# Down-projections' last unit summed earlier, raw products first at the beginning, and x copied by ScalarE

## The chip, the cores and the metric

The kernel runs on one core of a Trainium2 chip. The metric is the device time of one execution in microseconds. Three runs of the kernel before took 2900.92, 2905.70 and 2906.11 us; their median is 2905.7.

The engines go by the profile's names: PE is TensorE (PEld its loading of weights), DVE is VectorE, ACT is ScalarE, POOL is GpSimd, SP is SyncE, which issues nearly all loads.

## What is computed

x is 256 tokens of 1024 features in float32. Three blocks of a network follow each other: two layers of a conformer (convolution, then stick-breaking attention), a block with two kinds of attention, and a block with attention, a state-space branch and a mixture of experts. The change touches only the very first step of the program and the four feed-forward halves of the first block:

```python
def swiglu_ffn(h, w_in, w_out):
    gate, up = jnp.split(h @ w_in, 2, axis=-1)
    return (jax.nn.silu(gate) * up) @ w_out

def first_block(x, ...):
    for i in range(2):
        x = x + 0.5 * swiglu_ffn(rms_norm(x, g[0]), ffn_w_in[i, 0], ffn_w_out[i, 0])
        ...  # convolution (i = 0) or attention (i = 1)
        x = x + 0.5 * swiglu_ffn(rms_norm(x, g[2]), ffn_w_in[i, 1], ffn_w_out[i, 1])
```

w_in is 1024 x 5632 and w_out 2816 x 1024.

## The kernel before, in words

A plan of stages is run by every engine in the same order; the engines meet only at semaphores. x is held transposed in `xT`: 128 features by 256 tokens, eight such chunks. `Setup` loads x, lets PE transpose it into four banks (`turned` counts the banks, two chunks each), and DVE copies each bank into `xT` (L346), which raises `x_done`. For each pair of chunks `Norm.step` on DVE scales them by the gains into `hR` (L420, `h_ready`), and `Norm.act` on ACT squares them into `hT` (L411, `sq_ready`); `Norm.gather` (L428) adds the squares, `Norm.sum` is PE's sum over the partitions (L472), and its root and reciprocal give `rstd`.

Weights come through a ring of four slots. SP issues a unit's load as soon as PE has released the slot, which `w_used` counts, unit after unit through all stages.

`SevenUp` computes h @ w_in with seven products of half-sized blocks in place of eight. It takes 11 units of 2 MB. For each, DVE forms four sums of quarters of the weights (`combine`, L896 to L899, 128 x 1024 each; the last raises `combined`), and once per stage four sums of x's quarters (`take_turns`, L908 to L911; `turns`). A unit is two output chunks of 7 products each; a product is four matmuls of 128 x 128 by 128 columns in float32, and each matmul shows as two records in the trace. P1 and P2 read the weights and `hR` as they are; P3 reads a sum of weights and raw x; P6, P5, P7 and P4 read what was made of both (their tiles are `wrow`, `drow`, `hR` and `both`). In the first unit PE waits for the weights and for `combined`, then runs P1, P2 and P3 of both chunks, waits for `turns`, and runs the other four, with `Norm.sum` between the chunks.

`SevenDown` does the same for the second product, with 5 units of two pairs of chunks and a last one (unit 5) of one pair. `prepare` (L1192 to L1199) forms for unit j four sums of x's side and four of the weights'. It waits for the unit's load, for `w_used` of unit j - 2, whose work space it takes, and for the hidden chunks. For unit 5 the space is another: `drow`, `wrow`, `both` and the area from column 6144 on of `wk`. DVE prepares units 0 and 1 within the up-projection and 2 to 5 in `SevenDown.dve`, one behind the other. PE runs units 0 to 3 one by one; then it waits for units 4 and 5 both and takes them together, product by product, and `plus` (L1219) and L1227 to L1236 add each finished product to x behind it. In the second of the four down-projections an up-projection comes next but one, and DVE forms the sums of its unit 0 (`ahead`) after unit 5's; they lie in the space of unit 3.

DVE's first sums for the four up-projections start at 15, 358, 565 and 933 us, and its sums for unit 5 of the four down-projections at 211, 561, 776 and 1136 us.

Of the kernel before, what the change touches and what calls it, by code (L numbers as in the profile page):

```python
# [36 lines left out]
ACT, ALU, AX = mybir.ActivationFunctionType, mybir.AluOpType, mybir.AxisListType.X  # L37
# [197 lines left out]
class Stage:  # L235
# [11 lines left out]
    def banks_left(self, pe):  # L247
        pass
# [46 lines left out]
    def pe(self, pe):  # L295
        pass

    def act(self, act, chain):
        pass

    def dve(self, dve, chain):
        pass
# [5 lines left out]
class Setup(Stage):  # L308
# [16 lines left out]
        sp.dma_start(k.con[:, 0:FIRST], k.arg["constants"][:, 0:FIRST]).then_inc(self.ones_loaded, 16)  # L325

    def act(self, act, chain):
        k = self.k
        act.dma_start(k.par[:, :], k.arg["params"]).then_inc(k.par_loaded, 16)

    def pe(self, pe):
        k, nc = self.k, self.k.nc
# [9 lines left out]
    def dve(self, dve, chain):  # L342
        k, nc = self.k, self.k.nc
        for b in range(4):
            dve.wait_ge(self.turned, b + 1)
            nc.vector.tensor_copy(k.xT[:, 2 * b:2 * b + 2, :], pair(k.bank[:, 4 + b, :])).then_inc(k.x_done, 1)  # L346
            if b == 0:
                dve.wait_ge(k.par_loaded, 16)
            self.then.step(dve, chain, b)
        self.then.up.late = 1  # L350
        self.then.up.ahead(dve, chain)
        for n, (a, b) in enumerate((("final_g", "attn_norm_2"), ("final_norm_2", "norm_mix_w_3"))):
            chain(nc.vector.tensor_tensor(k.gains[:, n * KC:(n + 1) * KC], k.p(a, 0, KC), k.p(b, 0, KC), ALU.mult))


def pair(ap):
    return ap.rearrange("p (a n) -> p a n", a=2)
# [17 lines left out]
class Norm(Stage):  # L375
# [30 lines left out]

    def act(self, act, chain):
        k, nc = self.k, self.k.nc
        for b in range(4):
            act.wait_ge(k.x_done, self.x0 + b + 1)  # L410
            nc.scalar.activation(self.sq(b), k.xT[:, 2 * b:2 * b + 2, :], ACT.Square).then_inc(self.sq_ready, 1)  # L411
        act.wait_ge(self.mean_ready, self.at(self.mean_ready, 1))
        nc.scalar.activation(k.rstd[:, :], k.rstd[:, :], ACT.Sqrt).then_inc(self.root_ready, 1)

    def step(self, dve, chain, b):

        k, nc = self.k, self.k.nc
        dve.wait_ge(k.x_done, self.x0 + b + 1)
        for c in (2 * b, 2 * b + 1):
            last = nc.vector.tensor_scalar(k.hR[:, c, :], k.xT[:, c, :], self.g(c), None, ALU.mult)  # L420
        last.then_inc(self.h_ready, 1)
        if b >= 2:
            self.gather(dve, chain, b - 1)
# [265 lines left out]
class GatedUp(Stage):  # L689
# [56 lines left out]
    def t(self, n):  # L746
        a = (n % 4) * 2 * S
        return pair(self.k.wk[:, a:a + 2 * S])
# [26 lines left out]
class SevenUp(GatedUp):  # L775
# [25 lines left out]
    def s(self, j, n):  # L801
        a = (j % 2) * self.SW + (n if n < 3 else 2) * 1024
        return self.quarter(j, 0, 1) if n == 2 else self.k.wk[:, a:a + 1024].rearrange("p (c n) -> p c n", c=4)

    def b(self, half, t):
        return self.k.hR[:, 4 * half:4 * half + 4, t * P:(t + 1) * P]
# [26 lines left out]

    def pe(self, pe):
        k, nc, norm = self.k, self.k.nc, self.norm
        raw, made = (self.P1, self.P2, self.P3), (self.P6, self.P5, self.P7, self.P4)

        def products(n, which):
            j, m = n // 2, n % 2
            f = self.factors(j)  # L840
            for p in which:
                a, b = f[p]
                for c in range(4):
                    last = nc.tensor.matmul(k.bank[:, 2 * (n % 4) + p // 4, (p % 4) * P:(p % 4 + 1) * P],  # L844
                                            a[:, c, m * P:(m + 1) * P], b[:, c, :], start=c == 0, stop=c == 3)
            return last

        for j in range(self.UNITS):
            pe.wait_ge(self.loaded(j), self.loads(j))
            pe.wait_ge(self.combined, self.at(self.combined, j + 1))  # L850
            if j == 0:
                if self.at(self.scaled, -2) > 0:
                    pe.wait_ge(self.scaled, self.at(self.scaled, -2))
                for b in range(2):
                    norm.h_waits(pe, 2 * b)
                for m in range(2):
                    products(m, raw[:1])
                for b in range(2, 4):
                    norm.h_waits(pe, 2 * b)
                for m in range(2):  # L860
                    products(m, raw[1:])
                pe.wait_ge(self.turns, self.at(self.turns, 1))
                products(0, made).then_inc(self.up_ready, 1)
                norm.sum(pe)
                products(1, made).then_inc(k.w_used, 1)
                continue
            for m in range(2):
                n = 2 * j + m
                if self.at(self.scaled, n - 3) > 0:
                    pe.wait_ge(self.scaled, self.at(self.scaled, n - 3))  # L870
                if n == 2:
                    pe.wait_ge(norm.mean_ready, norm.at(norm.mean_ready, 1))
                products(n, raw + made).then_inc(k.w_used if m else self.up_ready, 1)
# [219 lines left out]
class SevenDown(Project):  # L1093
# [92 lines left out]
    def prepare(self, dve, chain, j):  # L1186

        v, a, b, t, s = self.k.nc.vector, self.quarter, self.b, self.turn, self.s
        dve.wait_ge(self.loaded(j), self.loads(j))
        dve.wait_ge(self.k.w_used, self.used(j - 2))  # L1190
        dve.wait_ge(self.by.hid_done, self.by.at(self.by.hid_done, FC // 2 + 2 * j + self.n(j)))
        chain.mark(v.tensor_tensor(t(j, 0), b(j, 0, 1), b(j, 0, 0), ALU.subtract))  # L1192
        chain(v.tensor_tensor(s(j, 0), a(j, 0, 1), a(j, 1, 1), ALU.add))
        chain.mark(v.tensor_tensor(t(j, 2), b(j, 1, 1), b(j, 0, 1), ALU.subtract))
        chain.mark(v.tensor_tensor(t(j, 1), b(j, 1, 1), t(j, 0), ALU.subtract))
        chain.mark(v.tensor_tensor(s(j, 2), a(j, 0, 0), a(j, 0, 1), ALU.subtract))
        chain(v.tensor_tensor(s(j, 1), s(j, 0), a(j, 0, 0), ALU.subtract))
        chain.mark(v.tensor_tensor(t(j, 3), b(j, 1, 0), t(j, 1), ALU.subtract))
        chain(v.tensor_tensor(s(j, 3), a(j, 1, 0), s(j, 1), ALU.subtract), self.made)  # L1199
# [13 lines left out]
    def dve(self, dve, chain):  # L1213
        k, v = self.k, self.k.nc.vector
        p1, u3, u4 = (self.sum(n) for n in range(3))
        x11, x12, x21, x22 = (k.xT[:, 4 * c:4 * c + 4, t * P:(t + 1) * P] for c in range(2) for t in range(T))

        def plus(out, p, x):
            return v.scalar_tensor_tensor(out, self.out(p), self.scale, x, ALU.mult, ALU.add)  # L1219

        for j in range(2, self.UNITS):
            self.prepare(dve, chain, j)
        if self.then.up:
            self.then.up.late = 1
            self.then.up.ahead(dve, chain)
        dve.wait_ge(self.p1_taken, self.at(self.p1_taken, 1))
        chain.mark(v.tensor_tensor(x11, x11, p1, ALU.add))  # L1227
        dve.wait_ge(self.out_ready, self.at(self.out_ready, 2))
        chain(plus(u3, self.P6, p1))
        dve.wait_ge(self.out_ready, self.at(self.out_ready, 3))  # L1230
        chain.mark(plus(u4, self.P5, u3))
        dve.wait_ge(self.out_ready, self.at(self.out_ready, 4))
        chain(plus(u3, self.P7, u3))
        chain.mark(v.tensor_tensor(x22, x22, u3, ALU.add))
        chain.mark(v.tensor_tensor(x21, x21, u3, ALU.add))
        chain(v.tensor_tensor(x12, x12, u4, ALU.add))  # L1236
        chain.mark(plus(x22, self.P5, x22))
        dve.wait_ge(self.out_ready, self.at(self.out_ready, 5))
        chain.mark(plus(x12, self.P3, x12))
        dve.wait_ge(self.out_ready, self.at(self.out_ready, 6))  # L1240
        plus(x11, self.P2, x11).then_inc(k.x_done, 2)
        self.then.step(dve, chain, 0)
        self.then.step(dve, chain, 1)
        dve.wait_ge(k.w_used, self.used(self.UNITS - 1))
        plus(x21, self.P4, x21).then_inc(k.x_done, 2)
        self.then.step(dve, chain, 2)
        self.then.step(dve, chain, 3)
# [1133 lines left out]
class SubNorm(Stage):  # L2381
# [29 lines left out]
    def square(self, act, chain):  # L2411
        k, nc = self.k, self.k.nc
        self.heads_out(act)
        chain(nc.scalar.activation(k.big[:, 0:8, :], k.big[:, 16:24, :], ACT.Square), self.squared)
# [1003 lines left out]
```

## Time and profile before

| | us |
|---|---|
| median of three runs | 2905.7 |
| the profiled execution | 2901.93 |
| its span | 2900.10 |
| PE busy | 2799.3 (97%) |
| DVE busy | 1421.7 (49%) |
| ACT busy | 472.2 (16%) |
| mean granted clock of PE | 0.988 |

All times below are counted from the start of the span. A timeline row gives start and duration, the engine and line, the operation with the tile it writes and those it reads, how many were merged, and in brackets the engine's idle time before it with what ended it. In the 40 slices of the page PE is at 9 tenths in nearly all; DMA is at 3 to 6 tenths until about 2220 us and at 9 from there on, in the stage of the experts.

### The profile page before, as it was taken

What the parts mean: (1) busy time and instruction counts of PE and PEld (TensorE: products, weight loads), DVE (VectorE), ACT (ScalarE), POOL (GpSimd) and SP (SyncE); (2) the same over time, 40 slices, a digit from 0 to 9 for tenths busy, and PEclk for the clock granted to TensorE, in tenths of its full rate; (3) what the DMA queues carried; (4) which work ended last, traced back from release to release, by engine and by line L of the source; (5) the groups of instructions that cost most, each with busy time, mean ns of one, the idle gap of its engine ahead of it and who ended that gap; (6) DMA issues with size and microseconds to landing.
All of it is one profiled execution on the core that took longest, in us unless ns stands there. A gap on an engine that the chain in (4) does not pass through costs nothing. (4 is left out here: it accounts for less than half of the span.)

```text
span 2900.1 us, 41051 instructions
## 1 busy us (share of the span) xinstructions
PE 2799.3 (97%) x17281; PEld 2264.6 (78%) x17281; DVE 1421.7 (49%) x2726; ACT 472.2 (16%) x953; POOL 0.2 (0%) x4
## 2 busy tenths in 40 slices
PE   7999899999999999999999999999997999999998
PEld 7998799999988999888888888888885434434343
DVE  7767687588555775542035337466103222223232
ACT  1001410010043100222010012344201000101001
POOL 0000000000000000000000000000000000000000
PEclk9999999999999999999999999999998999999999
DMA  7644155355354443546544444554553999999996
GB/s 225 207 151 151 46 162 175 131 175 174 117 131 146 157 164 113 133 113 156 155 145 147 158 109 110 155 144 125 138 156 136 427 426 426 426 426 427 425 427 288
DMA packets 370294, 594.80 MB, mean 205 GB/s; under 512 B 15680, under 2 KB 327264, under 8 KB 347488
## 3 DMA queue, kind: packets, MB, share of 16 engines
q1 hardware_dynamic: 365344, 588.01, 57.6%
q10 hardware_dynamic: 4800, 4.63, 0.6%
q8 instruction: 114, 1.87, 0.3%
q14 instruction: 36, 0.29, 0.0%
HBM read 591.52 MB, written 1.08 MB: 204 GB/s over the span
## 5 line engine op out<-in xcount | busy, mean ns | idle before, releaser
L3139 PE MATMUL bank<-ring,wk 128*64 128x512 f32 x1408 | 312.9, 597 | 6.0 <-DMA ring<-in_w_expert_gate 6.0
L844 PE MATMUL bank<-hR,ring 128*128 128x128 f32 x2112 | 267.9, 277 | 10.6 <-DVE wk L899 9.0
L3139 PEld LDWEIGHTS bank<-ring,wk 128*64 128x64 f32 x1408 | 99.8, 138 | 212.1 <-issue 212.1
L844 PEld LDWEIGHTS bank<-hR,ring 128*128 128x128 f32 x2112 | 252.8, 194 | 11.6 <-issue 9.4
L3236 DVE TENSOR_TENSOR hT<-bank,hT 128x512 f32<-128x512 f32 x92 | 63.6, 691 | 313.4 <-PE bank L3126 311.0
L3165 PE MATMUL bank<-big,wk 128*64 128x512 f32 x352 | 155.8, 595 | 15.1 <-ACT wk L3196 15.1
L733 PE MATMUL bank<-hR,ring 128*128 128x256 f32 x704 | 152.3, 379 | 0.0
L1157 PE MATMUL bank<-big,ring 128*128 128x128 f32 x1056 | 134.7, 284 | 15.6 <-DVE wk L1199 15.6
L733 PEld LDWEIGHTS bank<-hR,ring 128*128 128x128 f32 x704 | 133.8, 190 | 18.2
L2251 PE MATMUL bank<-big,ring 128*128 128x256 f32 x640 | 141.1, 379 | 1.5 <-ACT big L2733 1.0
L1157 PEld LDWEIGHTS bank<-big,ring 128*128 128x128 f32 x1056 | 129.3, 201 | 16.3 <-issue 16.3
L1038 PE MATMUL bank<-big,ring 128*128 128x256 f32 x608 | 134.5, 384 | 4.9 <-ACT big L1409 4.3
L2251 PEld LDWEIGHTS bank<-big,ring 128*128 128x128 f32 x640 | 121.4, 190 | 18.3 <-ACT big L2733 1.2
L1038 PEld LDWEIGHTS bank<-big,ring 128*128 128x128 f32 x608 | 116.9, 193 | 21.7 <-issue 4.7
L3165 PEld LDWEIGHTS bank<-big,wk 128*64 128x64 f32 x352 | 46.4, 137 | 108.3 <-issue 88.0
L2298 DVE TENSOR_TENSOR wk<-bank,wk 128x512 f32<-128x512 f32 x16 | 11.1, 692 | 216.8 <-ACT wk L2290 216.8
L1515 PE MATMUL bank<-hR,ring 128*128 128x256 f32 x512 | 114.5, 382 | 0.1
L2251 PE MATMUL bank<-hT,ring 128*128 128x256 f32 x512 | 113.3, 379 | 0.0
L2636 PE MATMUL bank<-hT,ring 128*128 128x256 f32 x512 | 113.0, 381 | 0.0
L1515 PEld LDWEIGHTS bank<-hR,ring 128*128 128x128 f32 x512 | 96.5, 191 | 13.9 <-DVE hR L420 0.9
L2636 PEld LDWEIGHTS bank<-hT,ring 128*128 128x128 f32 x512 | 97.2, 191 | 12.9
L2251 PEld LDWEIGHTS bank<-hT,ring 128*128 128x128 f32 x512 | 97.0, 190 | 13.0
(429 smaller groups left out, 4571.2 us busy)
## 6 DMA issues: line engine op xcount, KB each, us to landing
ring<-in_ffn_w_in SPq DMA_DIRECT2D x88, 1024.0 KB
ring<-in_w_expert_gate SPq DMA_DIRECT2D x44, 2048.0 KB
ring<-in_w_expert_up SPq DMA_DIRECT2D x44, 2048.0 KB
ring<-in_w_in SPq DMA_DIRECT2D x96, 512.0 KB
big<-in_w_expert_down SPq DMA_DIRECT2D x44, 1024.0 KB
ring<-in_ffn_w_out SPq DMA_DIRECT2D x40, 1024.0 KB
ring<-in_w_up SPq DMA_DIRECT2D x22, 1024.0 KB
hR<-in_w_expert_down SPq DMA_DIRECT2D x22, 1024.0 KB
```

Of the source, the lines that this page charges most:

```text
L733: last = nc.tensor.matmul(k.bank[:, n % 4, h * S:(h + 1) * S], w[:, c, h * 256 + m * P:h * 256 + (m + 1) * P], k.hR[:, c, :], start=c == 0 ...
L844: last = nc.tensor.matmul(k.bank[:, 2 * (n % 4) + p // 4, (p % 4) * P:(p % 4 + 1) * P], a[:, c, m * P:(m + 1) * P], b[:, c, :], start=c == ...
L1038: return k.nc.tensor.matmul(k.bank[:, self.banks[o // 2], (o % 2) * S:(o % 2 + 1) * S], w[:, c, o * P:(o + 1) * P], self.src[:, n, :], sta ...
L1157: last = k.nc.tensor.matmul(k.bank[:, self.BANK[p], m * P:(m + 1) * P], a[:, i, m * P:(m + 1) * P], b[:, i, :], start=j + i + m == 0, stop ...
L1515: last = nc.tensor.matmul(k.bank[:, bank, n * S:(n + 1) * S], w[:, c, n * P:(n + 1) * P], self.h[:, c, :], start=c == 0, stop=c == KC - 1)
L2251: last = nc.tensor.matmul(out, v[:, q, :], src[:, q, :], start=q == 0, stop=q == chunks - 1)
L2298: chain(nc.vector.tensor_tensor(k.wk[:, 3072:3072 + 2 * S], k.bank[:, 2 * (c % 2) + 1, :], both, ALU.mult))
L2636: last = nc.tensor.matmul(k.bank[:, n // 2, (n % 2) * S:(n % 2 + 1) * S], w[:, c, n * P:(n + 1) * P], k.hT[:, c, :], start=c == 0, stop=c ...
L3139: last = nc.tensor.matmul(k.bank[a:a + SLOTS, 2 + n, :], xg[:, c * P + a:c * P + a + SLOTS], self.weights(j, c, KC), start=c == 0, stop=c ...
L3165: last = nc.tensor.matmul(k.bank[a:a + SLOTS, 5 + h, :], ht[:, c * P + a:c * P + a + SLOTS], self.weights(j, c, 4)[:, h * 512:(h + 1) * 51 ...
L3236: return v.tensor_tensor(x, k.bank[:, self.PUT_BANKS[n], :], x, ALU.add)
```

## The change

Three edits:

- `Setup`: ACT copies the four banks into `xT` instead of DVE and squares each pair of chunks right behind its copy. The squares of this first norm move out of `Norm.act` into `Norm.square`; for all later norms nothing changes.
- `SevenUp.pe`, first unit: the wait for `combined` moves behind P1 and P2 of both chunks; P3 of both chunks follows it, then the wait for `turns` as before.
- `SevenDown.prepare`: unit 5 doesn't wait for `w_used` of unit 3 any more. Where sums for the next up-projection follow, this wait stands ahead of them instead.

```diff
 class Setup
     def act(self, act, chain):
-        k = self.k
+        k, nc = self.k, self.k.nc
         act.dma_start(k.par[:, :], k.arg["params"]).then_inc(k.par_loaded, 16)
+        for b in range(4):
+            act.wait_ge(self.turned, b + 1)
+            nc.scalar.activation(k.xT[:, 2 * b:2 * b + 2, :], pair(k.bank[:, 4 + b, :]), ACT.Copy).then_inc(k.x_done, 1)
+            self.then.square(act, b)
...
     def dve(self, dve, chain):
         for b in range(4):
-            dve.wait_ge(self.turned, b + 1)
-            nc.vector.tensor_copy(k.xT[:, 2 * b:2 * b + 2, :], pair(k.bank[:, 4 + b, :])).then_inc(k.x_done, 1)
...
 class Norm
     def act(self, act, chain):
-        for b in range(4):
-            act.wait_ge(k.x_done, self.x0 + b + 1)
-            nc.scalar.activation(self.sq(b), k.xT[:, 2 * b:2 * b + 2, :], ACT.Square).then_inc(self.sq_ready, 1)
+        if self.x0:
+            for b in range(4):
+                self.square(act, b)
...
+    def square(self, act, b):
+        act.wait_ge(self.k.x_done, self.x0 + b + 1)
+        self.k.nc.scalar.activation(self.sq(b), self.k.xT[:, 2 * b:2 * b + 2, :], ACT.Square).then_inc(self.sq_ready, 1)
...
 class SevenUp
     def pe(self, pe):
-        raw, made = (self.P1, self.P2, self.P3), (self.P6, self.P5, self.P7, self.P4)
+        raw, made = (self.P1, self.P2), (self.P3, self.P6, self.P5, self.P7, self.P4)
...
         for j in range(self.UNITS):
             pe.wait_ge(self.loaded(j), self.loads(j))
-            pe.wait_ge(self.combined, self.at(self.combined, j + 1))
-            if j == 0:
+            if j:
+                pe.wait_ge(self.combined, self.at(self.combined, j + 1))
+            else:
...
                 for m in range(2):
                     products(m, raw[1:])
+                pe.wait_ge(self.combined, self.at(self.combined, 1))
+                for m in range(2):
+                    products(m, made[:1])
                 pe.wait_ge(self.turns, self.at(self.turns, 1))
-                products(0, made).then_inc(self.up_ready, 1)
+                products(0, made[1:]).then_inc(self.up_ready, 1)
                 norm.sum(pe)
-                products(1, made).then_inc(k.w_used, 1)
+                products(1, made[1:]).then_inc(k.w_used, 1)
...
 class SevenDown
     def prepare(self, dve, chain, j):
-        dve.wait_ge(self.k.w_used, self.used(j - 2))
+        if j < self.UNITS - 1:
+            dve.wait_ge(self.k.w_used, self.used(j - 2))
...
     def dve(self, dve, chain):
         if self.then.up:
             self.then.up.late = 1
+            dve.wait_ge(k.w_used, self.used(self.UNITS - 3))
             self.then.up.ahead(dve, chain)
```

## Rows read from the trace of the kernel before

**Rows 1.** PE's waits, whole span: in all, times, longest (us)
```profile
PE bank L1157 <- DVE wk L1199: 15.6, 4, 3.9
...
PE bank L844 <- DVE wk L899: 9.0, 1, 9.0
```

**Rows 2.** Timeline, tail of the first down-projection: start, us, what, idle before
```profile
204.24 1.22 DVE L1199 TENSOR_TENSOR wk<-ring,wk 128x1024 f32<-128x1024 f32 x1
...
209.59 1.95 PE L1157 MATMUL bank<-hT,ring 128*128 128x128 f32 x16
211.75 0.29 DVE L1192 TENSOR_TENSOR drow<-big 128x128 f32<-128x128 f32 x1 [6.29 <-PE bank L1157]
...
214.61 0.68 DVE L1199 TENSOR_TENSOR wk<-ring,wk 128x512 f32<-128x512 f32 x1
...
221.61 1.06 PE L1157 MATMUL bank<-wrow,wk 128*128 128x128 f32 x8
```

**Rows 3.** One us of that tail: length, PE busy (records), clock, DMA share, GB/s
```profile
217.00:218.00 1.00, 1.00 (x7) 0.50 1.10 353
```

**Rows 4.** Timeline of PE, tails of the second and the fourth down-projection
```profile
559.62 1.95 PE L1157 MATMUL bank<-hT,ring 128*128 128x128 f32 x16
...
571.44 1.06 PE L1157 MATMUL bank<-wrow,wk 128*128 128x128 f32 x8
572.33 1.95 PE L1157 MATMUL bank<-hT,wk 128*128 128x128 f32 x16
...
1134.39 1.95 PE L1157 MATMUL bank<-hT,ring 128*128 128x128 f32 x16
...
1147.21 1.06 PE L1157 MATMUL bank<-wrow,wk 128*128 128x128 f32 x8
```

**Rows 5.** Window in the first down-projection: PE, PEld, DVE, ACT, POOL, clock, DMA, GB/s
```profile
193.00:196.00 3.00, 3.00 (x30) 3.00 (x29) 0.00 (x0) 0.00 (x0) 0.00 (x0) 1.00 0.00 0
```

**Rows 6.** Timeline of the beginning, Setup and first up-projection
```profile
8.69 0.69 DVE L346 COPY xT<-bank 128x512 f32<-128x512 f32 x1 [8.69 <-PE bank L338]
9.41 0.63 ACT L411 ACTIVATE hT<-xT 128x512 f32<-128x512 f32 x1 [6.95 <-DVE xT L346]
...
15.22 1.22 DVE L896 TENSOR_TENSOR wk<-ring 128x1024 f32<-128x1024 f32 x1
...
20.20 5.46 PE L844 MATMUL bank<-hR,ring 128*128 128x128 f32 x24 [8.99 <-DVE wk L899]
...
23.31 0.69 DVE L911 TENSOR_TENSOR both<-hR,wrow 128x512 f32<-128x512 f32 x1
...
28.28 1.06 PE L844 MATMUL bank<-wrow,wk 128*128 128x128 f32 x8
...
36.29 1.95 PE L844 MATMUL bank<-hR,ring 128*128 128x128 f32 x16
```

**Rows 7.** Window over PE's first products, columns as in group 5
```profile
20.20:25.70 5.50, 5.50 (x26) 5.50 (x27) 5.26 (x9) 0.00 (x0) 0.00 (x0) 1.00 1.10 349
```

**Rows 8.** ACT's copy of a whole bank, in the tail of group 2
```profile
219.68 0.60 ACT L1211 ACTIVATE wk<-bank 128x512 f32<-128x512 f32 x1 [39.18 <-PE bank L1157]
```

**Rows 9.** DMA queue of the loads, first 13 us: packets, MB, share
```profile
q1 hardware_dynamic: 2629, 3.41, 79.0%
```

**Rows 10.** Timeline of PE, two gaps elsewhere
```profile
298.37 30.50 PE L1348 MATMUL bank<-wk,hR 128*128 128x256 f32 x140 [1.36 <-DVE wk L1422]
...
1768.91 0.55 PE L1782 MATMUL bank<-con,wk 128*128 128x128 f32 x3 [1.98 <-DVE wk L1844]
```

**Rows 11.** Clock behind the second of them, columns as in group 3
```profile
1770.00:1772.00 2.00, 2.00 (x9) 0.50 1.20 303
```

**Rows 12.** SyncE's queue: the first load of the experts' weights
```profile
2222.91 1.07 SPq L3105 DMA_DIRECT2D ring<-in_w_expert_gate  x2
```

**Rows 13.** ACT: a table load, and a copy behind a square root
```profile
14.62 1.28 ACT L413 ACT_TABLE_LOAD   x1
...
33.77 0.26 ACT L880 ACTIVATE wk<-bank 128x128 f32<-128x128 f32 x1
```


## The prediction

> **What bounds the kernel now.** The page comes first: PE is by far the busiest engine, so a change pays only where PE stands idle or runs slowly. The next view is PE's list of waits. Its first entry is PE's products of the down-projections waiting for the last DVE sum (L1199): 15.6 us in 4 times, none over 3.9; its third is one wait of 9.0 us of the first up-projection for L899 [rows 1]. The change touches these two and nothing else on that list. The granted clock comes third, for what a wait costs besides itself.
>
> **The last unit of each down-projection, before.** PE ends unit 3 of the first one 1.95 us after 209.59, at about 211.5. DVE has been idle 6.29 us, and only then begins unit 5's eight sums: the first at 211.75, the last (0.68 us) at 214.61 [rows 2]. PE waits 3.90 us, since it takes units 4 and 5 together. The wait costs more than that. In the 218th us the granted clock is 0.50, that is 1.2 GHz instead of 2.4, after PE had been idle; PE then starts 7 matmul records in a us [rows 3]. So I take the whole cost from starts. From the last group of unit 3 (16 records) to the first product on wrow, past P1 (24) and P6's first half (16), are 56 records; at the steady pace, where 8 records take 0.89 us (571.44 to 572.33 [rows 4]), they need 56 x 0.1115 = 6.25 us. They took 221.61 - 209.59 = 12.02 here [rows 2], 571.44 - 559.62 = 11.82 in the second down-projection and 1147.21 - 1134.39 = 12.82 in the fourth [rows 4]; the third repeats the first to 0.01. The losses are 5.77, 5.57, 5.78 and 6.57, together 23.7 us: 15.6 of wait and 8.1 of half clock and restart. The granted clock is half in all four.
>
> **The same after.** Unit 5's eight sums no longer wait for unit 3's products. Unit 4's last sum begins at 204.24 and takes 1.22, so DVE is free at 205.46. The block lasted from 211.75 to 215.29 = 3.54 us, so it ends near 209.1, 2.4 us ahead of 211.5 [rows 2]. It stands beside unit 3's products in DVE's 6.29 us of idle time and costs nothing; if that cover were gone, PE would wait for what sticks out beyond 2.4 us. Its other conditions hold: unit 5's weights follow unit 1's release, and between 193 and 196 us the DMA engines stand still, all issued loads landed, before unit 4's sums begin [rows 5] (the three others look the same there); the last hidden unit is DVE's own earlier work, by the order of its code. No DMA is moved and SP's queue is passed by nothing. What is late next in the tail is PE itself, 28 products of unit 4 and as many halves of unit 5. I take the full 23.7; the lower bound is the waits alone, 15.6.
>
> The second down-projection has a further edit: the sums for the next up-projection (combine of its unit 0), until now behind unit 5's, get a wait of their own for unit 3's products. Behind it on DVE stand these four sums and then the first addition to xT. Before, they followed unit 5's last sum, on which PE's restart waits too. After, they begin at unit 3's end, which is PE's start of the tail: the same distance. P6's end (24 + 24 records, 5.4 us into the tail) comes later than theirs (4 sums of 1.22, as at L896 [rows 6], 5.0 with their waits), so DVE is back in step by the sum after it. Nothing for it.
>
> **The first up-projection, before.** The transposes end at 11.2. DVE copies x, scales it, adds squares, and starts unit 0's sums (combine, L896) at 15.22, straight behind its own L428; they end at 20.10. PE waits 8.99 us and starts at 20.20 [rows 6]. It runs P1, P2, P3 for both halves (48 records), waits for nothing, and starts the made products on wrow at 28.28; the turns of x (L908 to L911) had ended at 24.00. Unit 1 starts at 36.29 [rows 6]. From 20.2 to 25.7 PE starts 26 records in 5.5 us [rows 7], where 49 would fit at 0.1115 each, so the first stretch is at half speed although its granted clock is printed as 1.00. I therefore trust starts over the printed clock. The Trainium skill, "TensorE: Matmul & The Clock Gate", section "Part 1: The HAM clock gate (the "warmup" mystery)", warns that recorded clock events can be unreliable, and says that the slow state is the default and activity ends it. This row agrees with both; by the printed clock the slow stretch would not exist and an earlier start would gain more than I count.
>
> **The same after, step by step.** (a) ACT now copies x. A 128x512 copy out of a bank takes it 0.60 us [rows 8], its square 0.63, DVE's copy 0.69 [rows 6]. With about 0.05 for each wait a round is 1.3 us: the fourth copy ends at 8.69 + 3 x 1.3 + 0.6 = 13.2, DVE scales (0.62) and adds (0.68) to 14.6 and starts the sums 0.6 us earlier than at 15.22. The bounds: 0 if ACT's waits eat it, 2.7 (four DVE copies) if ACT were free. I take 0.6, since ACT's pace sets it. (b) The weights of unit 0: by 13.0 us queue q1 has moved 3.41 MB [rows 9]; x, the first constants and two 1.05 MB halves are 3.28 MB. So they are there at about 13, before DVE needs them. (c) PE starts P1 at about 13 and P2 after 13.9; these 32 records need 7.3 us at half speed, so they end between 17 and 20.3. The sums are ready at 19.5; P3 (16 records, 1.8 us) ends between 21.3 and 22.1. (d) Then PE waits for the turns, at 24.00 - 0.6 = 23.4. (e) From the first made product to unit 1 it took 36.29 - 28.28 = 8.0, so unit 1 starts at 31.4: 4.8 us earlier. (f) PE now meets a gap of 1.3 to 2.1 us that it did not have. A gap of 1.98 us before 1768.91 [rows 10] was followed by half clock [rows 11], and so was one of the same length at 246.7; one of 1.36 [rows 10] was not. The price of one such stretch is 5.57 - 3.90 = 1.7 us. I take it, by the rows nearest to 2 us: the start gives 4.8 - 1.7 = 3.1. Its bounds are 0 and 4.8 plus the 2.1 that DVE's copies could add at best.
> Behind it DVE's second combine ends at 28.92 - 0.6 = 28.3, before 31.4, and rstd moves with it. The other three up-projections have their sums before PE asks: there only the order of P2 and P3 changes, at no cost.
>
> **Whether the gain reaches the end.** In the last stage, the experts, DMA is nearly full by the page's slices. But its first load is issued at 2222.91 [rows 12], once the stages before are through, so this stage starts earlier as a whole, and its length stays.
>
> **The sum.** 23.7 + 3.1 = 26.8 us. The profiled execution took 2901.93, span 2900.10; it becomes 2875.1. The median of the three runs shown is 3.8 above it, and I predict for the median: 2905.7 - 26.8 = 2878.9 us.
>
> **Rivals.**
>
> R1, the clock holds at the start: the gap is nearer 1.3 than 2.1. For: P1 and P2 may be slow to the end; against: the two gaps near 2. Sum 23.7 + 4.8 = 28.5: 2877.2.
> R2, only the waits go: half clock comes in the tails anyway, from something other than the gap. Against: all four stretches lie at the gap and PE runs at 1.00 on both sides. Sum 15.6 + 3.1 = 18.7: 2887.0.
> R3, ACT loads a table at each change between copy and square: 7 changes x 1.28 us [rows 13] = 9.0 put the turns at 32.4 and unit 1 at 40.4, so the start loses 4.1: 23.7 - 4.1 = 19.6, 2886.1. Against: a copy follows a square root at 33.77 with no load between [rows 13]. The Trainium skill, "ScalarE: Activation LUTs", says that copy is in every table set; the trace agrees there.
> R4, the edit in the tails does nothing, since another condition holds unit 5's sums until unit 3 ends. DVE's wait in the trace is for PE, and the loads are done early, so little speaks for it. Sum 3.1: 2902.6.
> R5, slower: a PE without these pauses is granted half clock more often. It would sit in the dense stretch to 1161 us. The price is half of each us at 1.2 GHz; it decides from 54 us of additional half clock (26.8 lost), and 66 of it give 33 lost: 2911.9. Against: PE runs undisturbed at 1.00 for long dense stretches today.
>
> **How the numbers follow.** Forecast 0.47, R1 0.25, R2 0.12, R3 0.07, R4 0.03, R5 0.02; 0.04 for other small gaps that shift and move some half-clock stretch by 1.7 us either way. Runs of the kernel before spread 5.2 us (2900.92 to 2906.11). The range 2870 to 2888 takes in R1 less one spread, R2 and R3, and leaves out R4 and R5. About 0.2% (5.8 us) is what a measurement of this kernel can tell from no change; faster by more than that 0.95 (all but R4, R5), same 0.03, slower 0.02.
>
> **What the profile after would show.** In the tails: drow's sum near 205.5 - 4.8 in DVE, no PE wait for L1199, granted clock 1.00 there, 6.3 us from the last group of unit 3 to wrow. At the start: PE's first product near 13, a wait of PE for L911 of 1.3 to 2.1 us, unit 1 at 31.4 (33.1 with half clock); ACT without table loads between its copies. The prediction is wrong if a wait of over 1 us for L1199 stays, if the clock is half in the tails, or if the gain is there at 1160 us and gone at 2230.

## The result and the profile after

The median went from 2903.76 us (four runs, 2900.92 to 2906.11) to 2878.65 us (four runs, 2876.68 to 2878.84). The ratio is 0.9912 with a 95% interval of 0.9895 to 0.9930: faster, by 25.1 us. The prediction was 2878.9 us, in a range of 2870 to 2888. The profiled execution took 2876.68 us and its span 2874.9, 25.2 less than before, where the sum had said 26.8. In one more series, on another occasion, the changed kernel's median was 2876.41 (2874.79 to 2878.20) against 2901.24 before.

First the waits of PE. Of the two entries that the change was about [rows 1], the tails' 15.6 us are gone from the list. In place of the 9.0 us stand two shorter waits in the first up-projection: 2.3 us for the scaled x (L427) and 1.9 us for the turns (L922). Columns: in all, times, longest.

```profile
PE bank L851 <- DVE hR L427: 3.9, 4, 2.3
PE bank L1795 <- DVE wk L1857: 3.8, 2, 2.0
...
PE bank L851 <- DVE both L922: 2.5, 4, 1.9
```

**The tails.** The timeline of the first down-projection after, the same places as [rows 2] (L1204 and L1211 are L1192 and L1199 of before, L1168 is L1157):

```profile
199.22 1.22 DVE L1211 TENSOR_TENSOR wk<-ring,wk 128x1024 f32<-128x1024 f32 x1
200.47 0.29 DVE L1204 TENSOR_TENSOR drow<-big 128x128 f32<-128x128 f32 x1
...
203.34 0.69 DVE L1211 TENSOR_TENSOR wk<-ring,wk 128x512 f32<-128x512 f32 x1
...
204.56 1.95 PE L1168 MATMUL bank<-hT,ring 128*128 128x128 f32 x16
...
206.35 2.84 PE L1168 MATMUL bank<-big,ring 128*128 128x128 f32 x24
...
210.82 1.06 PE L1168 MATMUL bank<-wrow,wk 128*128 128x128 f32 x8
```

Unit 5's sums follow unit 4's last one without a break and end at 204.03. PE ends unit 3 at 206.35 and starts the tail there. From the last group of unit 3 to wrow it now takes 210.82 - 204.56 = 6.26 us, where the sum had 6.25 and before 12.02. The clock holds. Per us: length, PE busy (records), clock, DMA share, GB/s:

```profile
206.00:207.00 1.00, 1.00 (x11) 1.00 0.00 0
...
208.00:209.00 1.00, 1.00 (x11) 1.00 0.63 134
```

**The beginning.** The rows that answer to [rows 6]:

```profile
8.87 0.60 ACT L332 ACTIVATE xT<-bank 128x512 f32<-128x512 f32 x1 [6.39 <-PE bank L342]
9.50 0.63 ACT L420 ACTIVATE hT<-xT 128x512 f32<-128x512 f32 x1
...
12.33 0.58 ACT L332 ACTIVATE xT<-bank 128x512 f32<-128x512 f32 x1
...
13.68 5.47 PE L851 MATMUL bank<-hR,ring 128*128 128x128 f32 x32 [2.29 <-DVE hR L427]
14.30 1.23 DVE L907 TENSOR_TENSOR wk<-ring 128x1024 f32<-128x1024 f32 x1
...
19.23 2.05 PE L851 MATMUL bank<-hR,wk 128*128 128x128 f32 x16
...
22.40 0.69 DVE L922 TENSOR_TENSOR both<-hR,wrow 128x512 f32<-128x512 f32 x1
...
23.15 1.16 PE L851 MATMUL bank<-wrow,wk 128*128 128x128 f32 x8 [1.86 <-DVE both L922]
...
31.26 1.95 PE L851 MATMUL bank<-hR,ring 128*128 128x128 f32 x16
```

ACT copies in 0.60 and 0.58 us and squares behind each copy, the sums start at 14.30 instead of 15.22, PE starts at 13.68 instead of 20.20, the turns end at 23.09 and unit 1 starts at 31.26 instead of 36.29.

**A ledger.** A record of PE in one trace can be set against the same record in another. The table gives by how much a kernel's record starts ahead of that of the kernel before, at seven places: the first product of unit 1 (36.29 in before), the first products behind the four down-projections (235.91, 585.73, 800.49, 1161.50), one in the last block (2041.13), one in the experts (2244.45), and the end of the span. Each row is one profiled execution. The work behind 1161 us is the same in all of them. The record at 2041.13 is the one behind a wait that comes up again below.

| kernel | unit 1 | 236 | 586 | 800 | 1161 | 2041 | 2244 | end |
|---|---|---|---|---|---|---|---|---|
| after | 5.03 | 10.79 | 16.25 | 22.02 | 28.57 | 27.75 | 25.14 | 25.2 |
| after_again | 4.78 | 10.54 | 15.02 | 20.79 | 27.35 | 26.80 | 24.31 | 24.5 |
| after_third | 3.58 | 9.35 | 13.81 | 19.58 | 26.14 | 25.58 | 23.03 | 23.2 |
| tail_only | -0.30 | 5.47 | 11.62 | 17.39 | 23.94 | 23.65 | 23.50 | 23.7 |
| order_only | 4.04 | 2.74 | 2.75 | 2.75 | 2.76 | 2.75 | 2.78 | 3.0 |
| copy_only | 1.55 | 1.54 | 2.13 | 2.13 | 2.12 | 2.35 | 2.17 | 2.4 |
| start_only | 5.20 | 5.20 | 1.45 | 0.64 | 0.26 | 0.00 | -0.12 | -0.1 |
| filled_wait | -0.19 | 1.43 | 3.69 | 5.32 | 7.73 | 7.06 | 6.63 | 6.8 |
| late_sums | 5.21 | 6.41 | 7.46 | 10.30 | 12.38 | 10.41 | 10.21 | 10.4 |
| turns_first | 5.95 | 11.71 | 15.49 | 21.72 | 28.74 | 26.76 | 24.28 | 24.5 |
| later_9 | 3.19 | 8.95 | 13.42 | 19.18 | 25.74 | 25.04 | 24.89 | 24.6 |
| later_18 | 1.02 | 6.78 | 9.95 | 15.71 | 22.27 | 21.64 | 21.48 | 21.3 |
| shifted_code | 5.29 | 11.06 | 17.22 | 22.99 | 29.54 | 28.94 | 28.70 | 28.7 |

The first row already says what the total hides: 28.6 us were gained by 1161 us, and 3.4 of them were lost behind it, in stages that the change doesn't touch.

### The profile page after: what moved, and what is told of

The parts are those of the page before. It is cut to its first block and busy times, and to the rows that moved or that the text cites. A ratio compares the mean times of both kernels' runs of the same rounds, so it can differ in the third digit from the quotient of the medians.

```text
span 2874.9 us, 41046 instructions
## 1 busy us (share of the span) xinstructions
PE 2796.7 (97%) x17281; PEld 2260.9 (79%) x17281; DVE 1419.8 (49%) x2722; ACT 474.7 (17%) x957; POOL 0.2 (0%) x4
## 5 line engine op out<-in xcount | busy, mean ns | idle before, releaser
L2264 PEld LDWEIGHTS bank<-big,ring 128*128 128x128 f32 x640 | 121.4, 190 | 18.3 <-ACT big L2746 1.2
L1049 PEld LDWEIGHTS bank<-big,ring 128*128 128x128 f32 x608 | 116.8, 193 | 21.8 <-issue 4.7
L1168 PE MATMUL bank<-big,ring 128*128 128x128 f32 x1056 | 127.7, 275 | 0.0
L1168 PEld LDWEIGHTS bank<-big,ring 128*128 128x128 f32 x1056 | 122.7, 192 | 0.0
```

Source lines behind the costliest of these rows:

```text
L1049: return k.nc.tensor.matmul(k.bank[:, self.banks[o // 2], (o % 2) * S:(o % 2 + 1) * S], w[:, c, o * P:(o + 1) * P], self.src[:, n, :], sta ...
L1168: last = k.nc.tensor.matmul(k.bank[:, self.BANK[p], m * P:(m + 1) * P], a[:, i, m * P:(m + 1) * P], b[:, i, :], start=j + i + m == 0, stop ...
L2264: last = nc.tensor.matmul(out, v[:, q, :], src[:, q, :], start=q == 0, stop=q == chunks - 1)
```

## The experiments

### The edits one by one

The changed kernel once more, as it is.

> The changed kernel once more, nothing altered. The first traces agree to 0.1 us in which gains have come by where: 5.0 us behind the first up-projection, 28.6 by 1161 us, and then 3.4 are lost by 2250 us. Theory 1 (the loss is chance: half-clock stretches of the second and third block fall differently in each execution): the first two figures repeat within 0.5 us, the loss from 1161 us on comes out otherwise, anywhere from -5 to +5 us. Theory 2 (the loss is the change's, given back later): it is again 3.4 within 0.5 us, with the same half-clock stretches at 1786 and 2015 us.

Unit 1 at 4.78, 27.35 at 1161 us, and then 2.8 lost. The first figure repeats to 0.25, the second only to 1.2 (1.0 of it arose between 236 and 586 us, where the half-clock stretches fell differently), and the loss behind 1161 us is there again, with the half-clock stretch at 2016 us. That spoke for theory 2.

The tails' edit alone:

```diff
 def prepare(self, dve, chain, j):
-    dve.wait_ge(self.k.w_used, self.used(j - 2))
+    if j < self.UNITS - 1:
+        dve.wait_ge(self.k.w_used, self.used(j - 2))
 ...
+        dve.wait_ge(k.w_used, self.used(self.UNITS - 3))
         self.then.up.ahead(dve, chain)
```

> Only the edit of the down-projections. Forecast by the prediction: 23.7 us gained by the end of the fourth, in steps of 5.8, 5.6, 5.8 and 6.6, no PE wait for the last sum in the tails, no half clock there, and nothing gained before 200 us. Rival (only the wait goes, the half clock comes anyway): 15.6. The time is 0.9918 of before if it all lasts, 0.9946 by the rival.

The gains between the places of the table are 5.77, 6.15, 5.77 and 6.55, together 24.2; 0.6 of the second came before its tail, from a shorter half-clock stretch at 337 us. Taken from the last records of unit 3 to the end of the down-projection, the four tails gain 5.77, 5.56, 5.77 and 6.56, together 23.7 as forecast, and the same, within 0.01, in the seven other traces that have this edit and nothing put ahead of unit 5's sums. Only 0.4 is lost later. The ratio is 0.9925 (0.9908 to 0.9941), median 2879.25. The rival of 15.6 is out.

The order of the products alone:

```diff
-        raw, made = (self.P1, self.P2, self.P3), (self.P6, self.P5, self.P7, self.P4)
+        raw, made = (self.P1, self.P2), (self.P3, self.P6, self.P5, self.P7, self.P4)
 ...
-            pe.wait_ge(self.combined, self.at(self.combined, j + 1))
-            if j == 0:
+            if j:
+                pe.wait_ge(self.combined, self.at(self.combined, j + 1))
+            else:
```

> Only the order in the first unit of the up-projections: P1 and P2 ahead of the wait for the sums. DVE still copies x, so the turns are ready at 24.0 as before, and unit 1 starts at 24.1 + 8.0 = 32.1: 4.2 us gained, if the half clock does not follow PE's wait for the turns; 2.5 if it does. Rival (the order brings little by itself, it needs the faster sums): under 1 us.

```profile
13.55 6.68 PE L844 MATMUL bank<-hR,ring 128*128 128x128 f32 x32 [2.28 <-DMA ring<-in_ffn_w_in]
...
24.14 1.16 PE L844 MATMUL bank<-wrow,wk 128*128 128x128 f32 x8 [1.86 <-DVE both L915]
...
32.25 1.95 PE L844 MATMUL bank<-hR,ring 128*128 128x128 f32 x16
```

PE starts its raw products at 13.55, waits 1.86 us for the turns, and unit 1 starts at 32.25: 4.04, where 4.2 were expected. But at the first tail 1.3 of it is given back, and the ratio is 0.9996 (0.9987 to 1.0006).

```profile
212.00:214.00 2.00, 2.00 (x11) 0.50 1.10 349
214.00:216.00 2.00, 2.00 (x11) 0.50 0.65 204
```

The old wait in the tail is still there in this kernel, and half clock behind it lasted 6.8 us from 210.7 on instead of 3.4.

ACT's copy alone:

```diff
 class Setup, def act
+        for b in range(4):
+            act.wait_ge(self.turned, b + 1)
+            nc.scalar.activation(k.xT[:, 2 * b:2 * b + 2, :], pair(k.bank[:, 4 + b, :]), ACT.Copy).then_inc(k.x_done, 1)
+            self.then.square(act, b)
 class Setup, def dve
-            dve.wait_ge(self.turned, b + 1)
-            nc.vector.tensor_copy(k.xT[:, 2 * b:2 * b + 2, :], pair(k.bank[:, 4 + b, :])).then_inc(k.x_done, 1)
```

> Only ACT's copy of x and its squares. The sums end 0.6 to 0.9 us earlier, and PE, which then has only them to wait for, starts 0.6 to 0.9 us earlier; unit 1 starts at 35.4 to 35.7. Rival (the four copies of 0.69 us come off DVE's path in full): 2.7 us.

```profile
19.17 5.04 PE L851 MATMUL bank<-hR,ring 128*128 128x128 f32 x24 [7.88 <-DVE wk L906]
...
34.74 1.95 PE L851 MATMUL bank<-hR,ring 128*128 128x128 f32 x16
```

PE starts 1.03 earlier, a little above the expected 0.6 to 0.9, and reaches unit 1 1.55 earlier; the other 0.5 is that the slow pace at the start of PE's work ended 0.5 us sooner in its run of products (24 records in 5.04 instead of 5.46 us). The rival's 2.7 is out: ACT's rounds of copy and square set the pace. Ratio 0.9996 (0.9987 to 1.0006).

Both edits of the start without the tails':

> The two edits of the start together, without the tails'. Alone the order gave 4.0 and the copy 1.55 us at unit 1; together 5.0 as in the first trace of after (3.5 if half clock follows PE's wait for the turns). By 235 us this may shrink, as the order's 4.0 did to 2.7, since the half clock in the first tail can last 6.8 us instead of 3.4. From 1161 us on: nothing lost if the loss hangs on the time of arrival (this one comes 5 us earlier than before, not 24 to 29), 3 lost if it hangs on the start's edits.

Little of the gain lasts in this trace. The 5.20 at unit 1 are still whole behind the first down-projection, 1.45 behind the second and 0.26 at 1161 us. The loss has two places. The first is the convolution between 236 and 301 us, where 2.6 us go (0.3 comes back at 347 us) and the change alters nothing:

```profile
293.20 33.34 PE L1359 MATMUL bank<-wk,hR 128*128 128x256 f32 x140 [3.07 <-DVE wk L1433]
```

In the kernel before, half clock followed a wait of 1.97 us ahead of 246.71 (from 247.6 on, 3.4 us), and PE then waited 1.36 us at this line [rows 10]. Here no half clock followed the first wait, so PE came to L1359 early, waited 3.07 us for DVE, and half clock of 6.8 us (from 292.2 on) followed that wait. The second place is the tails, whose waits are still four of 3.9. The first tail loses nothing, the other three lose 1.5, 0.8 and 0.4 us against before. In the second and third the half clock is longer:

```profile
562.00:564.00 2.00, 1.46 (x7) 0.50 1.09 360
564.00:566.00 2.00, 2.00 (x11) 0.50 1.07 341
566.00:568.00 2.00, 2.00 (x11) 0.50 0.05 14
```

It lasts 6.8 us at 561.8 and at 776.9, where the trace of before had 3.4 each time. The profiled execution took 2902.0 us, where ten executions lie between 2897.0 and 2903.6; over all of them the ratio is 0.9988 (0.9979 to 0.9998), about 3 us. So the start's gain is real, but how much of it lasts changes from execution to execution with the half clock behind PE's later waits. That is so in the changed kernel too, whose tails have no waits: between 236 us and the second tail after loses 0.1, after_again and after_third lose 1.1. Both of these have the wait of 3.07 us in the convolution, after has 1.38. From 1161 us on start_only loses 0.3, so the start's edits alone don't bring the later loss.

### What a wait costs

In the kernel before, PE's wait in the tails was filled with work that no one reads:

```diff
+        for _ in range(16):
+            k.nc.tensor.matmul(k.bank[:, 2, 0:P], k.c("ones"), k.c("ident"), start=True, stop=True)
         for j in (end, end + 1):
             self.ready(pe, j)
```

> The kernel before, with 16 matmuls that no one reads (ones by identity, into a free bank) on PE between unit 3 and its wait for the last sums, in all four down-projections. They take 32 x 0.1115 = 3.6 us of the wait of 3.9, so PE still starts the tails when the sums are there. If the half clock comes from PE's idleness, it goes, and the four tails lose 3.9 each instead of 5.8, 5.6, 5.8 and 6.6: 8.1 us gained by 1161 us. Rival (the half clock comes from something else at that place, such as the loads that start there): nothing gained.

```profile
211.57 3.74 PE L1177 MATMUL bank<-con 128*128 128x128 f32 x32
215.64 2.92 PE L1157 MATMUL bank<-big,ring 128*128 128x128 f32 x24 [0.34 <-DVE wk L1201]
...
216.00:217.00 1.00, 1.00 (x11) 1.00 1.11 357
...
218.00:219.00 1.00, 1.00 (x11) 1.00 1.10 347
```

PE does 32 records more in each tail and the kernel is 7.9 us ahead at 1161 us (7.73 + 0.19 at unit 1); expected were 8.1. Not all of the 7.9 comes from the tails: these gain 1.62, 1.42, 1.63 and 2.42, together 7.1, and 0.8 come from a half-clock stretch at 340 us that lasted 3.4 us instead of 6.8. Each tail gains 0.25 less than forecast; 0.17 of it is that the records on both sides of the wait start 4.18 us apart, 4.07 beyond the steady pace, where the profile lists 3.90 as idle. Ratio 0.9975 (0.9966 to 0.9985). The loads that start at this place run as before (1.10 in the DMA column), and the clock stays at 1.00. In none of the four tails is there half clock. So it comes from PE's idleness, and a wait of 3.9 us costs 5.6 to 6.6.

In the changed kernel, DVE's sums of unit 5 were put off:

```diff
         for j in range(2, self.UNITS):
+            if j == self.UNITS - 1:
+                for _ in range(4):
+                    chain(v.tensor_tensor(w, w, w, ALU.max))  # w: 1024 columns of wk that nothing reads here
             self.prepare(dve, chain, j)
```

> The changed kernel with four idle sums of 128x1024 (5.0 us) on DVE ahead of unit 5's. In the trace of after, unit 5's block ends at 204.0 and PE needs it at 206.4, so the cover is 2.3 us. If it is this cover that makes the edit free, PE waits 2.7 us again in each tail: 10.8 us lost in all, and up to 6.8 more where half clock follows a gap of 2.7. Rival (DVE's block isn't what PE is near to waiting for, another 3 us of cover exist): under 1 us lost.

```profile
PE bank L1168 <- DVE wk L1211: 10.8, 4, 2.7
...
200.29 5.00 DVE L1236 TENSOR_TENSOR wk<-wk 128x1024 f32<-128x1024 f32 x4
...
209.03 4.24 PE L1168 MATMUL bank<-big,ring 128*128 128x128 f32 x24 [2.70 <-DVE wk L1211]
...
771.36 2.92 PE L1168 MATMUL bank<-big,ring 128*128 128x128 f32 x24 [2.70 <-DVE wk L1211]
```

Four waits of 2.7 us, 10.8 in all, as the cover of 2.3 us says. At 1161 us the kernel is 16.2 us behind after (12.38 against 28.57), so 5.4 went to half clock. Tail by tail it gains 4.6, 4.6, 2.9 and 4.5 us less than after: half clock followed three of the four equal waits, and behind the third (771.36) the 24 records took 2.92 us instead of 4.24. Ratio to before 0.9965 (0.9952 to 0.9977), against 0.9912 for the changed kernel.

### What the start waits for

The changed kernel with the turns ahead of DVE's smaller work:

```diff
 class Setup, def dve, in the loop, at b == 0
+                for n, (g, h) in enumerate((("final_g", "attn_norm_2"), ("final_norm_2", "norm_mix_w_3"))):
+                    chain.mark(nc.vector.tensor_tensor(k.gains[:, n * KC:(n + 1) * KC], k.p(g, 0, KC), k.p(h, 0, KC), ALU.mult))
 class Norm, def dve
-        self.gather(dve, chain, 3)
-            self.up.take_turns(dve, chain)
+            self.up.take_turns(dve, chain, lambda: self.gather(dve, chain, 3))  # the gather behind the turns
```

> The changed kernel with DVE's work behind the first combine in another order: the two products for the gains go into DVE's idle time at its first step, and the last addition of squares goes behind the turns, in all four up-projections. If PE's wait at the start is for DVE's row of work, the turns end 0.4 + 0.7 = 1.1 us earlier, PE's wait of 1.9 shrinks to 0.8, and unit 1 starts 1.1 us earlier; the other three up-projections keep their times. Rival (P3, or the sum of squares that now comes later, is late next): 0, or a loss in the others where the sum of squares feeds the mean.

```profile
19.43 0.69 DVE L921 TENSOR_TENSOR drow<-hR 128x512 f32<-128x512 f32 x1
...
20.20 1.95 PE L853 MATMUL bank<-hR,wk 128*128 128x128 f32 x16
...
21.48 0.69 DVE L924 TENSOR_TENSOR both<-hR,wrow 128x512 f32<-128x512 f32 x1
...
22.23 1.16 PE L853 MATMUL bank<-wrow,wk 128*128 128x128 f32 x8
```

The turns start right behind the sums, the wait of 1.86 us is 0.27 (read on PE's row of weight loads; in this execution P1 and P2 were also slower and ended later), and unit 1 starts at 5.95 in the table, 0.9 beyond after and 1.2 beyond after_again. So DVE's row of work is what the start waits for, as the prediction had it. Over the whole kernel it can't be told from the changed one: median 2875.91 (2874.31 to 2877.41) against 2876.41 in the same hours.

### The 3 us that are lost later

The changed kernel a third time:

> The changed kernel a third time. In two executions 3.4 and 3.0 us were lost between 1161 and 2250 us, 0.9 and 0.5 of it by 2041 us, and the half-clock stretches at 2015 and 2183 us were there in both, but not in the kernel with the tail edit alone. If this belongs to the kernel: again about 3 with the same two stretches. If it is where the execution falls against the clock's changes: another figure.

2.9 lost again behind 1161 us (26.14 to 23.23), so it belongs to the kernel. This execution also shows what the prediction had counted on at the start: PE waits 1.86 us for the turns in after and here, but here half clock follows (from 24.0 on, 3.4 us), and unit 1 starts 3.58 us ahead of before, where the two others have 5.03 and 4.78.

```profile
22.00:24.00 2.00, 1.04 (x9) 1.00 1.10 348
24.00:26.00 2.00, 2.00 (x12) 0.51 1.10 349
26.00:28.00 2.00, 2.00 (x14) 0.64 1.12 351
```

Then the question was whether the loss hangs on the time at which the execution arrives there. Two kernels are the changed one with idle matmuls at the start:

```diff
                 pe.wait_ge(self.turns, self.at(self.turns, 1))
+                for _ in range(18 if not norm.x0 else 0):  # 9 in the other
+                    nc.tensor.matmul(k.bank[:, 7, 0:P], k.c("ones"), k.c("ident"), start=True, stop=True)
                 products(0, made[1:])
```

> The changed kernel with 18 matmuls that no one reads (ones by identity, free bank) on PE at the first made products: everything behind is 4.0 us later, so the gain at 1161 us is 28.6 - 4.0 = 24.6 where the changed kernel has 28.6 (26.1 to 28.6 in three executions), close to the 23.9 of the tail edit alone, which then lost nothing. If what the changed kernel loses between 1161 and 2250 us hangs on when it comes there, little is lost here (under 0.5 us) and the time is that of the changed kernel within 1 us, although PE had 4.0 us more to do. If the loss has nothing to do with that, 3 are lost again, and the time is 4 us longer.

> The same with 9 matmuls, 2.0 us. If the loss of the second and third block hangs on the time of arrival: between 0 and 3 us of it. If not: 3 lost, 2 us longer than the changed kernel.

The gains at 1161 us are 22.27 (18 matmuls) and 25.74 (9). At a record ahead of the experts (2223.10 in before), later_18 has lost 2.3 us of that and later_9 2.4, against 2.5 in after and 2.2 in after_again and after_third; in tail_only it is 0.3. So the time of arrival doesn't matter and that theory is out. The end shows less, 1.0 and 1.2, since 1.5 us came back between 2223 and 2244 us, where after loses 0.9: PE's wait for the experts' first weights is 4.0 us instead of 5.2, and the half clock behind it lasts 3.4 us instead of 6.8. Their medians are 2879.15 and 2877.77.

What the traces with the loss have in common is one stretch. In the last block DVE idles before L2796 (L2809 after) with nothing in the trace that it waits for, and then PE waits for the sums behind it. In after:

```profile
1992.85 1.38 DVE L2809 TENSOR_SCALAR wk<-wk,par 128x256 f32<-128x256 f32 x4 [4.36 <-issue]
...
2013.38 2.00 PE L2705 MATMUL bank<-wk 128*128 128x64 f32 x16 [1.13 <-DVE wk L2849]
...
2014.00:2016.00 2.00, 2.00 (x15) 1.74 (x15) 0.05 (x1) 0.00 (x0) 0.00 (x0) 0.84 1.10 321
2016.00:2018.00 2.00, 2.00 (x8) 1.79 (x7) 1.57 (x4) 0.82 (x2) 0.00 (x0) 0.50 1.21 291
```

The same place in before, DVE and PE:

```profile
2020.61 1.38 DVE L2796 TENSOR_SCALAR wk<-wk,par 128x256 f32<-128x256 f32 x4 [4.01 <-issue]
...
2041.13 2.00 PE L2692 MATMUL bank<-wk 128*128 128x64 f32 x16 [0.77 <-DVE wk L2836]
...
2042.00:2044.00 2.00, 2.00 (x18) 1.90 (x17) 0.29 (x1) 0.00 (x0) 0.00 (x0) 1.00 1.03 305
2044.00:2046.00 2.00, 2.00 (x11) 1.77 (x10) 1.90 (x4) 0.84 (x2) 0.00 (x0) 1.00 1.21 292
```

DVE idles 4.36 us in after and 4.01 in before, PE waits 1.13 instead of 0.77, and in after the clock falls to 0.50 right behind. The record by record comparison puts 0.36 us on the longer wait and 1.68 on the half clock (the gain is 28.11 ahead of the wait and 26.07 at 2050 us in before's time), 2.0 of the 2.5 that are lost by 2223 us. In after_again, after_third, turns_first and the two delayed kernels DVE idles 4.34 or 4.35 and half clock follows too; in tail_only, order_only, copy_only, start_only, filled_wait and late_sums it idles 3.99 to 4.01 and the clock stays up. One more thing splits the traces in the same way, a half-clock stretch from about 2183 us on: it lasts 20.5 us in the six with the loss and 17.1 in all others. What differs between these groups on DVE is how many instructions come before. Counted in the traces, 2631 records of DVE and its sequencer stand ahead of this place in before, 2627 in tail_only, copy_only and start_only, 2639 in late_sums, and 2623 in the six with the loss. So the last experiment moved only that:

```diff
 class Setup, def dve
+        for _ in range(16):
+            chain(nc.vector.memset(k.small[:, 0:1], 0.0))
         for b in range(4):
```

> The changed kernel with 16 writes of one column on DVE before the first bank of x is there, when DVE has nothing to do: no work is moved or delayed, only DVE's later instructions stand 16 places further on, as they do in late_sums. In all traces with both edits and nothing added on DVE, DVE idles 4.35 us at L2796 (its line of before) around 1993 us, where before, tail_only, start_only and late_sums have 4.00; PE then waits 1.13 us instead of 0.77 and half clock follows at 2015. If the extra 0.35 us hangs on where DVE's instructions lie, it is 4.00 here, the half clock at 2015 goes, and of the 3 us lost after 1161 us only about 1 is left: the span is 2 us under that of after. If it hangs on something else: 4.35 again and 3 lost.

```profile
1991.67 1.38 DVE L2811 TENSOR_SCALAR wk<-wk,par 128x256 f32<-128x256 f32 x4 [4.00 <-issue]
...
2012.20 2.00 PE L2707 MATMUL bank<-wk 128*128 128x64 f32 x16 [0.77 <-DVE wk L2851]
...
2014.00:2016.00 2.00, 2.00 (x13) 1.00 1.18 318
2016.00:2018.00 2.00, 2.00 (x11) 1.00 1.21 290
```

DVE idles 4.00, PE waits 0.77, the clock holds, and of 29.54 us at 1161 us only 0.9 are lost. The stretch at 2182 us is back to 17.1. The median of four runs is 2873.51 (2873.26 to 2874.98), and three of the four lie below the lowest of the nine runs of the changed kernel (2874.79 to 2878.84); ratio to before 0.9903 (0.9886 to 0.9920). It is the fastest kernel of this study, with 16 instructions more than the changed one. Of its lead over after in the trace (28.7 against 25.2) some 2.5 us are the smaller loss; the other 1.0 arose ahead of 1161 us, where executions of one kernel differ as much. That the position of DVE's instructions decides over the 4.35 or 4.00 us is shown by this run together with the groups above; why it does (how they reach the engine, where they lie) is not, and the trace names nothing for the 4 us.

## Why the prediction was right, step by step

- **The cost of the tails' waits, taken from starts and not from the wait alone.** Right. The tails gain 5.77, 5.56, 5.77 and 6.56 in after against 5.77, 5.57, 5.78 and 6.57; filled_wait splits them nearly as the prediction did (8.1 us of half clock and restart, of which 7.1 come back in the tails).
- **The cover of unit 5's sums.** Right: they end at 204.03, 2.3 us ahead of PE, forecast 2.4, and late_sums shows what lies beyond. The second down-projection's new wait cost nothing: its tail gains 5.56 where its stall had been 5.57.
- **ACT's copies.** The round was forecast at 1.3 us and was 1.15 to 1.17 (9.50 to 10.65, 10.65 to 11.80 for the squares): the 0.05 for each wait was not there, and a copy starts 0.09 us before the square ahead of it ends (11.19 against 11.28). The sums start 0.92 earlier, not 0.6. No table was loaded in between, so R3 is out.
- **Unit 1 at 31.4.** It was 31.26. (By the prediction's own numbers 31.4 is 4.9 us earlier, not 4.8.)
- **The half clock behind PE's wait for the turns.** The mis-sized term in this execution: forecast 1.7 us lost, measured 0. It differs between executions, though: the same wait of 1.86 us was followed by half clock in after_third and not in after, order_only and shifted_code. In after_again the wait was 1.31 and nothing followed. R1 was the case that came, as to this term, but for another reason than it gave: the wait was near its upper bound, and the clock held all the same.
- **What reaches the end.** Wrong. "This stage starts earlier as a whole" holds for the experts, but not the tacit step that all stages in between keep their length: they gave back 3.4 us. Of these, 2.0 are a longer wait of PE and the half clock behind it in the last block, which hang on where DVE's instructions lie; 0.9 are lost at the experts' first products. The case for small gaps had 0.04 and 1.7 us.
- **The sum.** On the profiled execution: forecast 26.8; the trace gives 5.03 + 23.54 - 3.35 = 25.22. Two terms that are wrong by about +1.9 (the start) and -3.4 (later) partly cancelled. The median came out within 0.3 us of the forecast because the base was taken at 2905.7, 1.9 above the median that four runs give. The mechanism of both gains was right; the last two microseconds of agreement were luck.

## What to carry to other kernels

Price a wait of TensorE by the starts of its records around it, down to where the steady pace is back: here 3.9 us of waiting cost 5.6 to 6.6. A gain far ahead of TensorE's other waits may not reach the end: without the tails' edit the start's 5 us were about 3 over ten runs and 0.3 in one trace. A part went where an earlier TensorE only waits longer for another engine, a part to longer half clock behind waits that had not changed. And to see whether an expected gain arrived, set the same record of two traces against each other at several places; the total alone would have confirmed a sum of which two terms were wrong.

## What the runs showed of the hardware that was not expected

- Sixteen writes that no one needs, put where DVE was idle, took 0.35 us off an idle time of DVE 1990 us later. PE's loss there went from 2.0 us to nothing (after, after_again and after_third lose 3.4, 2.8 and 2.9 us behind 1161 us in all, shifted_code 0.9).
- PE's wait of 1.12 or 1.13 us in the last block was followed by half clock in all six traces that have it; one of 0.77 to 0.79 at the same place was followed by none in the eight others.
- The convolution's wait of 1.97 us, the same in all 14 traces, was followed by half clock in seven of them. In the other seven PE came early to its next wait, which was 3.06 or 3.07 us instead of 1.36 to 1.38, and half clock of 3.4 or 6.8 us followed there in six.
- The same wait of 3.9 us was followed by 3.4 us of half clock in one execution and by 6.8 in another (first tail: 3.4 from 216.9 on in before, 6.8 from 210.7 on in order_only), which makes a part of the spread of some 5 us between runs of the kernel before plausible; that this is its cause wasn't tested.
